# Reordering the first stage of a streaming trunk step: norm, conditioning and first projections

## What is computed

```python
mod = jax.nn.silu(c) @ w_ada + b_ada            # c: one row for the prompt, one for the sample
sh1, sc1, g1, sh2, sc2, g2 = jnp.split(mod, 6, axis=-1)
y = xf * lax.rsqrt(jnp.mean(xf * xf, axis=-1, keepdims=True) + EPS)   # rmsnorm, times gain
h = h * (1 + scale[:, None, :]) + shift[:, None, :]                   # modulate
rq, rk, rv, rg, aq, ak, av = split_in(h @ w_in)
```

## Time and profile before

| | us |
|---|---|
| time, median of 3 runs | 1336.36 |
| lowest and highest run | 1335.98 and 1337.28 |
| the profiled execution, its own time | 1338.92 |
| its span, from first to last instruction | 1337.1 |
| PE busy in the span | 1257.2 (94%) |
| DVE busy | 840.5 (63%) |
| ACT busy | 524.1 (39%) |
| POOL busy | 517.7 (39%) |

### The profile page before, as it was taken

How to read it: one execution, slowest core, us unless ns; L and a number is a source line. 1 busy time by engine, 2 the same in 40 slices (tenths; PEclk the granted TensorE clock), 3 DMA queues, 4 the chain that set the end, 5 groups by cost and what they waited for, 6 DMA issues and landing times.

```text
span 1337.1 us, 22495 instructions
## 1 busy us (share of the span) xinstructions
PE 1257.2 (94%) x8537; PEld 1181.3 (88%) x8537; DVE 840.5 (63%) x1519; ACT 524.1 (39%) x1063; POOL 517.7 (39%) x313
## 2 busy tenths in 40 slices
PE   5879999999999899779999999999999999999995
PEld 2548988988988899769999999999999999899995
DVE  5978558477396636996666666666666368682305
ACT  5644344345345523543343333334333322333432
POOL 0002032131042433444534535344352577665770
PEclk9999999999999899989999999999999999999998
DMA  9412223032222413203222232322222898685981
GB/s 366 168 53 80 72 73 125 24 120 78 92 90 89 151 36 115 99 32 116 102 109 98 99 114 90 122 98 99 106 91 85 310 365 302 217 325 200 321 274 45
DMA packets 74393, 185.56 MB, mean 139 GB/s; under 512 B 7424, under 2 KB 39744, under 8 KB 74048
## 3 DMA queue, kind: packets, MB, share of 16 engines
q1 hardware_dynamic: 72640, 183.63, 38.3%
q10 hardware_dynamic: 1664, 0.72, 0.2%
HBM read 150.14 MB, written 34.19 MB: 138 GB/s over the span
## 4 chain that ended last, share of the span: by engine, by line
PE 67%; DVE 12%; DMA 6%; POOL 5%; issue 5%; ACT 3%; SPq 2%; DVEq 0%; ACTq 0%; POOLq 0%
PE bank L2166 32%; PE bank L1893 13%; PE bank L2206 9%; PE bank L2142 5%; DMA w_raw<-in_w_units 4%; POOL w_extra L1295 2%; PE bank L2013 2%; DVE std L1530 1%; DVE ada_out L1332 1%; PE bank L1983 1%; POOL w_more L1295 1%; PE bank L1998 1%; POOL w_hl L1295 1%; POOL w_hl L1256 1%; DMA ada_d<-in_w_ada_t 1%
## 5 line engine op out<-in xcount | busy, mean ns | idle before, releaser
L1893 PE MATMUL bank<-act_hl,w_hl 128*128 128x362 f32 (+1 forms) x1368 | 256.5, 336 | 0.1
L1893 PEld LDWEIGHTS bank<-act_hl,w_hl 128*128 128x128 f32 x1368 | 223.3, 188 | 9.4 <-issue 7.1
L1183 POOL TENSOR_TENSOR w_hl<-w_raw,w_hl 128x1024 fp32r<-128x1024 f32 x21 | 50.2, 2392 | 345.1 <-ACT w_hl L727 345.1
L2206 PE MATMUL bank<-u_hl,w_more 128*128 128x362 f32 (+1 forms) x672 | 116.3, 332 | 4.4 <-POOL w_more L1295 4.1
L2166 PE MATMUL bank<-x_blocks_a,w_hl 128*128 128x272 f32 x864 | 114.0, 291 | 5.8 <-issue 5.8
L2206 PEld LDWEIGHTS bank<-u_hl,w_more 128*128 128x128 f32 x672 | 113.5, 191 | 5.1 <-POOL w_more L1295 4.5
L2166 PEld LDWEIGHTS bank<-x_blocks_a,w_hl 128*128 128x128 f32 x864 | 111.6, 191 | 6.1 <-issue 6.0
L2166 PE MATMUL bank<-x_blocks_b,w_hl 128*128 128x272 f32 x864 | 112.7, 288 | 1.4 <-ACT x_blocks_b L993 1.1
L2166 PE MATMUL bank<-x_blocks_a,w_ext 128*128 128x272 f32 x840 | 109.5, 289 | 4.3 <-DVE prod_sb L1635 2.4
L2166 PEld LDWEIGHTS bank<-x_blocks_b,w_hl 128*128 128x128 f32 x864 | 109.8, 188 | 2.3 <-DVE up_b L1640 1.3
L2166 PEld LDWEIGHTS bank<-x_blocks_a,w_ext 128*128 128x128 f32 x840 | 106.8, 189 | 5.0 <-issue 2.6
(11 more groups left out here) (229 smaller groups left out, 2290.2 us busy)
## 6 DMA issues: line engine op xcount, KB each, us to landing
w_raw<-in_w_units SPq DMA_DIRECT2D x139, 512.0 KB, 4.5
ada_w<-in_w_ada_t SPq DMA_DIRECT2D x36, 512.0 KB, 3.6
u_hl<-u_dram SPq DMA_DIRECT2D x44, 362.0 KB, 5.6
u_dram<-acc SPq DMA_DIRECT2D x22, 544.0 KB, 2.7
u_dram<-up_b SPq DMA_DIRECT2D x22, 544.0 KB, 2.7
ada_d<-in_w_ada_t SPq DMA_DIRECT2D x16, 512.0 KB, 5.8
u_hl<-u_dram SPq DMA_DIRECT2D x22, 364.0 KB, 7.7
xm<-in_x_t SPq DMA_DIRECT2D x2, 1448.0 KB, 13.8
```

Source lines behind the costliest of these rows:

```text
L1183: pool.tensor_tensor(w_hl[:, slot, 1], w_raw[:, slot], w_hl[:, slot, 0].bitcast(F32), ALU.subtract).then_inc(wl_ready, 1)
L1893: ins = pe.matmul(bank[c][:, 0:m], w_hl[:, slot, w, k, :], act_hl[:, x, k, a:a + m], start=(pas == 0 and i == 0), stop=(pas == 2 and i == ...
L2206: ins = pe.matmul(bank[o][:, 0:m], w_down(q)[:, w, o, :], u_hl[:, q % U_RING, x, 0:m], start=(f == pas == 0), stop=(f == FT - 1 and pas == 2))
```

## The change

`std_flat` now takes the roots without the two spare columns, so that all 1088 reciprocals lie side by side. A list X_STEPS takes the place of X_ORDER: rows 0 and 1 by chunks, rows 2 to 6 in one step over all tokens (instructions of 1024 and 64 columns), row 7 by chunks. ACT shifts in place only, and PE waits for that (`x_shifted`); the rounded high part becomes a separate copy of a whole row (`x_hi`), some steps later. On DVE the dots of tiles 4, 5, 6 and 7 move ahead, between and behind the three reciprocals. On PE row 7 is worked chunk by chunk as its chunks come, the ninth product waits for one result copied out instead of seven, and the nine transpositions go to three banks without a wait between them, after the eighth result is copied; DVE copies them in three instructions. ACT copies results in the order in which they are made.

```diff
--- before.py
+++ after.py
@@ -75,8 +75,9 @@
 W_RING = W_MORE + 3 + W_EXTRA
 ADA_LOADS = tuple(range(11))
 ADA_PLACE = {m: m % 11 for m in range(16)}
-X_ORDER = ([(0, 0), (1, 0), (0, 1), (1, 1), (2, 0), (2, 1), (0, 2), (1, 2), (2, 2)]
-           + [(k, c) for k in range(3, KT) for c in range(3)])
+X_STEPS = ([(k, lo, hi) for ks, c in (((0, 1), (0, 1)), ((0, 1), (2,))) for k in ks for lo, hi in
+            [(CHUNKS[i][0], sum(CHUNKS[i])) for i in c]] + [(k, 0, T) for k in range(2, KT - 1)]
+           + [(KT - 1, a, a + n) for a, n in CHUNKS])
 LATE = 4
 OUT_JOBS = ([(o, n) for o in range(1, 8) for n in (0, 1)] + [(o, n) for o in (4, 5, 3, 7) for n in (2, 3)]
@@ -228,6 +229,7 @@
+        X_LAST = [max(i for i, step in enumerate(X_STEPS) if step[0] == k) for k in range(KT)]
@@ -265,6 +267,7 @@
+        x_shifted = sem("x_shifted")
@@ -742,15 +745,19 @@
                 act.activation(std[:, c, 0:n], bank[at or SUM_BANK[c]][:, 0:n], ACT.Sqrt, bias=eps_sb[:, 0:1],
                                scale=1.0 / width).then_inc(std_ready, 1)
-            def shift_x(k, c):
-
-                act.wait_ge(x_scaled, X_ORDER.index((k, c)) + 1)
-                for in_place in (False, True):
-                    for o, tok, m, part in pieces(c):
-                        x = xm[:, k, tok:tok + m]
-                        ins = act.activation(x if in_place else act_hl[:, 0, k, tok:tok + m], x, ACT.Identity,
-                                             bias=mod[:, 2 * k + 1, part:part + 1])
-                ins.then_inc(hi_ready, 1)
+            def shift_x(i):
+
+                k, lo, hi = X_STEPS[i]
+                act.wait_ge(x_scaled, i + 1)
+                for o, tok, m, part in token_parts(lo, hi):
+                    x = xm[:, k, tok:tok + m]
+                    ins = act.activation(x, x, ACT.Identity, bias=mod[:, 2 * k + 1, part:part + 1])
+                ins.then_inc(x_shifted, 1)
+
+            def x_hi(k):
+
+                act.wait_ge(x_shifted, X_LAST[k] + 1)
+                act.activation(act_hl[:, 0, k, :], xm[:, k, :], ACT.Copy).then_inc(hi_ready, 1)
             act.sem_inc(state_stored, 32)
             act.sem_inc(wh_ready, 3)
@@ -768,7 +775,7 @@
             def x_root(c):
                 n = CHUNKS[c][1]
                 act.wait_ge(sum_ready, c + 1)
-                act.activation(std[:, c, 0:n], bank[X_SUM_BANK[c]][:, 0:n], ACT.Sqrt, bias=eps_sb[:, 0:1],
+                act.activation(std_flat[:, CHUNKS[c][0]:sum(CHUNKS[c])], bank[X_SUM_BANK[c]][:, 0:n], ACT.Sqrt, bias=eps_sb[:, 0:1],
                                scale=1.0 / D).then_inc(std_ready, 1)
             act.wait_ge(cond_loaded, 16)
@@ -780,8 +787,14 @@
             x_squares(2)
             x_root(2)
             act.wait_ge(sq_used, 3 * KT)
-            for k, c in X_ORDER:
-                shift_x(k, c)
+            for i in range(len(X_STEPS)):
+                shift_x(i)
+                if 6 <= i <= 10:
+                    x_hi(i - 6)
+                if i == 10:
+                    x_hi(5)
+                    x_hi(6)
+            x_hi(KT - 1)
             def evac(n_chunk, at, dst, func=ACT.Copy, scale=1.0):
@@ -790,20 +803,27 @@
                 act.activation(dst[:, a:a + n], bank[at][:, 0:n], func, scale=scale).then_inc(act_evac, 1)
             for c in range(3):
-                act.wait_ge(gemm_ready, c + 1)
-                for o, t, n, part in pieces(c):
-                    ins = act.activation(ak[:, t + P * part:t + P * part + n], bank[c][:, o:o + n], ACT.Copy)
-                ins.then_inc(act_evac, 1)
-            act.wait_ge(act_evac, 3)
+                for u in range(3):
+                    if u == c == 2:
+                        continue
+                    act.wait_ge(gemm_ready, 3 * c + u + 1)
+                    for o, t, n, part in pieces(c):
+                        if u == 0:
+                            ins = act.activation(ak[:, t + P * part:t + P * part + n], bank[c][:, o:o + n], ACT.Copy)
+                        elif part == 0:
+                            a, n = CHUNKS[c]
+                            ins = act.activation((rv, aq)[u - 1][:, a:a + n], bank[3 * u + c][:, 0:n], ACT.Copy,
+                                                 scale=(1.0, ATT_SCALE)[u - 1])
+                    ins.then_inc(act_evac, 1)
+            split_weights(3, [3])
+            act.wait_ge(act_evac, 7)
             act.dma_start(pk_t, ak[:, S_PROMPT - P:S_PROMPT]).then_inc(stored, 16)
             act.dma_start(sk_t, ak[:, T + P - S_SAMPLE:T + P]).then_inc(stored, 16)
-            for c in range(3):
-                evac(3 + c, 3 + c, rv)
-            split_weights(3, [3])
-            for c in range(3):
-                evac(6 + c, (6, 7, 0)[c], aq, scale=ATT_SCALE)
+            act.wait_ge(gemm_ready, 9)
+            a, n = CHUNKS[2]
+            act.activation(aq[:, a:a + n], bank[0][:, 0:n], ACT.Copy, scale=ATT_SCALE).then_inc(act_evac, 1)
             split_weights(4, [4])
-            act.wait_ge(av_tok_ready, NB)
+            act.wait_ge(av_tok_ready, 3)
             act.dma_start(pv, av_tok[:, 7, :]).then_inc(stored, 16)
             act.dma_start(sv, av_tok[0:S_SAMPLE, 9, :]).then_inc(stored, 16)
@@ -1365,12 +1385,19 @@
                                   ALU.add, ALU.mult).then_inc(vec_ready, 1)
                 dve.wait_ge(vec_ready, k + 1)
-            def scale_x(*parts):
-
-                for k, c in parts:
-                    for o, tok, m, part in pieces(c):
+            def first_invert(c):
+
+                at = std_flat[:, CHUNKS[c][0]:sum(CHUNKS[c])]
+                dve.wait_ge(std_ready, c + 1)
+                then_wait(dve.reciprocal(at, at))
+
+            def scale_x(*steps):
+
+                for i in steps:
+                    k, lo, hi = X_STEPS[i]
+                    for o, tok, m, part in token_parts(lo, hi):
                         x = xm[:, k, tok:tok + m]
-                        ins = dve.scalar_tensor_tensor(x, x, scale_n[:, 0, k, part:part + 1], std[:, c, o:o + m],
+                        ins = dve.scalar_tensor_tensor(x, x, scale_n[:, 0, k, part:part + 1], std_flat[:, tok:tok + m],
                                                        ALU.mult, ALU.mult)
                     ins.then_inc(x_scaled, 1)
@@ -1380,40 +1407,42 @@
                                   ALU.subtract).then_inc(lo_ready, 1)
             dve.wait_ge(silu_c_ready, 1)
-            for m in range(4):
+            for m in range(5):
                 first_ada_dots(m)
-            invert(0, 0)
+            first_invert(0)
+            for m in (5, 6):
+                first_ada_dots(m)
+            first_invert(1)
             first_vectors(0)
-            scale_x((0, 0))
+            scale_x(0, 1)
             first_vectors(1)
-            scale_x((1, 0))
-            first_ada_dots(4)
-            first_ada_dots(5)
-            invert(1, 1)
-            scale_x((0, 1), (1, 1))
+            scale_x(2, 3)
+            first_invert(2)
+            scale_x(4, 5)
             first_vectors(2)
-            scale_x((2, 0), (2, 1))
-            invert(2, 2)
-            scale_x((0, 2), (1, 2), (2, 2))
-            for k in range(3, KT):
+            scale_x(6)
+            first_ada_dots(7)
+            first_vectors(3)
+            scale_x(7)
+            for k in range(4, KT):
                 first_ada_dots(2 * k)
                 first_ada_dots(2 * k + 1)
                 first_vectors(k)
-                scale_x(*[(k, c) for c in range(3)])
-
-            dve.wait_ge(x_scaled, 3 * KT)
+                scale_x(*[i for i, step in enumerate(X_STEPS) if step[0] == k])
+
+            dve.wait_ge(x_scaled, len(X_STEPS))
             dve.sem_inc(norm_applied, 3)
-            dve.wait_ge(hi_ready, 3 * (KT - 1))
-            for k in range(KT - 1):
+            for k in range(KT):
+                dve.wait_ge(hi_ready, k + 1)
                 x_lo(k)
-            dve.wait_ge(hi_ready, 3 * KT)
-            x_lo(KT - 1)
-
-            for b in range(NB):
-                t, n = BLOCKS[b]
-                dve.wait_ge(av_t_ready, b + 1)
-                dve.tensor_copy(av_tok[0:n, b + (b == NB - 1), :], bank[(3, 6)[b % 2]][0:n, 0:P]).then_inc(av_tok_ready, 1)
+
+            for i, (b0, b1) in enumerate(((0, 4), (4, 8))):
+                dve.wait_ge(av_t_ready, i + 1)
+                dve.tensor_copy(av_tok[:, b0:b1, :], bank[(3, 6)[i]][:, :].rearrange("p (b d) -> p b d", b=4)).then_inc(
+                    av_tok_ready, 1)
+            dve.wait_ge(av_t_ready, 3)
+            dve.tensor_copy(av_tok[0:S_SAMPLE, NB, :], bank[4][0:S_SAMPLE, 0:P]).then_inc(av_tok_ready, 1)
             def mask_and_max(j, b):
@@ -1924,14 +1953,6 @@
             def nothing(s):
                 pass
-            def values_by_token(s):
-
-                t, n = BLOCKS[s]
-                if s >= 2:
-                    pe.wait_ge(av_tok_ready, s - 1)
```

(31 more changed lines are left out.)

## The result

The changed kernel takes 1324.51 us (median of 4 runs, 1324.09 to 1325.66), against 1336.49 us for the kernel before on the same chips. The ratio is 0.9911, with a 95% interval from 0.9899 to 0.9922: 12.0 us faster, where 11.6 were forecast. Two later measurements, each beside the kernel before, gave 11.1 and 10.5 us. Its profiled execution took 1324.34 us, with a span of 1322.5.

A forecast was written before the change was run, and what follows sets the result against it. DVE's chain bounds the first stage, though PE leads overall. Unit 3 starts 11.6 us earlier (5.4 from DVE's chain, the rest PE's last row, clock, ninth product and transpositions, less POOL's hold): 1336.36 to 1324.8 us, range 1321.5 to 1329.0.

The forecast's parts named there:

- DVE up to the last row: DVE's chain before unit 3: idle pieces go and whole rows cost 1.40 us, so row 7 starts 5.4 us earlier.
- PE and the last row: PE before unit 3: the 4.46 us wait goes, row 7 takes 5.15 us from 73.3, transpositions end at 84.9.
- the reason given for it: PE's row 7: charged 5.15 us because the lower clock followed an idle PE that would no longer be idle.
- What is late next: Low parts on DVE before unit 3: held by POOL's subtraction, they end at 86.1, after the transpositions; unit 3 starts then.
- one hold by POOL: DVE's low parts: POOL's subtraction for unit 3's weights takes a turn among them, moving their end 2.4 us from 83.7.
- rival 1: Before unit 3: no hold between POOL and the low parts, unit 3 at 84.9, 1323.6 us; chance 0.20.
- Behind unit 3: From unit 3's start to the end: the change costs nothing, and weight loads move with the rest.
- rival 2: DVE's whole rows: they bring nothing because columns cost all, 1.3 us lost, 1326.1 us; chance 0.10.
- Rival 3: The heads: a load or table of the first head becomes late, time stays at about 1336 us; chance 0.04.
- Rival 4: DVE's dots before roots: tile 5 or 6 landing late delays the chain, slower if tile 6 lands after 39.0; chance 0.02.

The follow-up runs named there:

- dots_behind: Changed kernel, but DVE's dots of tiles 4 to 6 go back behind the roots; 1330.97 us.
- rows_by_chunks: Changed kernel, but rows 2 to 6 are scaled and shifted chunk by chunk instead of whole; 1328.44 us.
- by_turns: Changed kernel, but the nine transpositions take turns in two banks again, each waiting for the copy before the last; 1330.47 us.
- subtraction_later: Changed kernel, but POOL's first subtraction also waits for six low parts, so it comes up during the seventh; 1325.53 us.
- late_wait_for_low: Changed kernel, but PE waits for low parts only behind unit 3's first eight products and first scores; DVE copies values before its last low part; 1324.04 us.
- no_subtraction: Changed kernel, but POOL leaves out its first subtraction, so the low part of unit 3's weights is zero; 1323.12 us.
- tile_6_late: Changed kernel, but SP issues the loads of conditioning tiles 6 and 7 behind the three weight units; 1329.75 us.
- last_row_whole: Changed kernel, but row 7 is scaled, shifted and waited for as a whole, like rows 2 to 6; 1327.33 us.
- early_and_late: Kernel of late_wait_for_low, but ACT loads its table early by a one-column Silu and SP issues conditioning tile 4 before x chunk 1; 1324.02 us.

## Why the prediction was right

**DVE up to the last row.** Right step by step: reciprocal 0 at 22.52 (22.4 forecast), vectors 0 at 32.5 (32.4), rows 3, 4 and 7 scaled at 44.01, 51.03 and 72.13 (44.0, 51.0, 72.1). A whole row costs 1.39 (1.40). The run dots_behind shows that the order of the dots is worth some 5 us at unit 3 (of the 5.7 to 6.1 us, 0.9 are a root that came later), and rows_by_chunks that whole rows are worth 1.3.

**PE and the last row.** Row 7 was forecast to start at 73.3 and started at 73.42; the ninth product at 78.86 (78.5), the end of the transpositions at 84.96 (84.9), nine of them in 1.15 us (1.3). One thing came otherwise: row 5, from 61.02 us, took 6.84 us, so the stretch at the lower clock was still there, after an idle PE of 1.89 us. It was hidden, since row 6 was not ready before 68.06. In the third run of the changed kernel it came in row 6 (the granted clock is 0.53 of full speed from 69 to 71 us, 0.62 from 71 to 73 and 1.00 after), which pushed row 7 back by 1.2 us; rows 6 and 7 took 11.72 us together, the transpositions ended at 85.80, and unit 3 started there, no later than in the others. So row 7 itself was spared in all three profiles, but the reason given for it was only half right. PE's waits of 1.9 us did not go; they moved to rows 5 and 6, and in by_turns, subtraction_later and late_wait_for_low two of them were followed by rows of 5.15 us. Which row is slowed differs between profiles of one kernel, and that it was none that mattered is partly luck.

**What is late next.** The low parts with one hold by POOL were forecast to end at 86.1; DVE's next instruction starts at 85.80 and PE at 86.22. Two small errors cancel in it: the hold was charged 2.4 us and cost 2.15, and PE started 0.34 us after the last low part ended (74.02 + 11.86 = 85.88), where the sum had nothing. That the hold is POOL's is shown by no_subtraction (84.80, the forecast of rival 1 being 84.9). The Trainium skill, "SBUF — State Buffer", section "SBUF: two separate sides", has the two blocking each other for whole instructions, and a low part of 3.44 instead of 1.28 us, 2.16 more, with a subtraction of 2.4 in between, agrees. DVE's copies of values, forecast at most 0.2 us late, ended at 87.27, before the first scores began at 87.74.

**Behind unit 3.** "Nothing" was right within what the profiles can tell: the rest of the span is 1236.3 to 1239.8 us for the changed kernel and 1239.45 for the one before. A change of 1 us there could not be seen. That the first median hit the forecast to 0.3 us is therefore luck in part: the second and third are 1.2 and 2.0 us above 1324.8. What carries the prediction is the start of unit 3, 11.4 to 11.9 us earlier where 11.6 was forecast.

**The rivals.** Rival 1 (no hold) and rival 2 (columns cost all) fall by the profile and by a run each. Rival 3 (the heads give it back) falls by the time. Rival 4, dots in front of roots made late by a load, did not happen, but tile_6_late shows its mechanism: 3.6 us of load are 3.6 us at unit 3.

**The reserve.** Why does PE's part of the change look small when it is undone? Because two paths end almost together. The last row by chunks and the separate rounding move PE's path, and each can be undone alone for 0 to 0.5 us. The transpositions without waits are another matter: undone, they cost 2.5 us, since the copies that they wait for stand behind the low parts. The ninth product's wait was not undone alone. Before the change that path ended at 97.65, with the low parts finished at 89.09: PE's edits brought it down to the low parts, and the last microsecond of them is now slack. How much each of them took off on the way is not shown, since no run undoes two together.

## What to carry to other kernels

Instructions that wait for nothing belong in front of those that wait for another engine; count then when their own data land, since a queue that works in order passes on each microsecond of a late load (3.6 here). When several edits shorten one path until it meets another, undoing one of them tells little: read where both paths end. And measure from an event behind the first loads, not from the start of the span: here that took the spread of the changed kernel from 0.42 us to 0.04. Before a POOL instruction is moved into a run of DVE instructions with two inputs in SBUF, add their durations up, as one after the other.

## What was not expected of the hardware

Who waits for whom, POOL or DVE, followed a pattern that I can't explain. In eight profiles POOL's subtraction came up during the sixth of the eight low parts (as at 80.09 above), and the seventh was held. In four (tile_6_late, last_row_whole, subtraction_later and the third run of the changed kernel) it came up during the seventh, and the eighth ran at once, so that POOL's instruction lasted 3.9 to 4.6 us. It is not simply that the last instruction of a run goes first, or that copies stand behind it: in late_wait_for_low and early_and_late, two of the eight, only seven low parts stood in front of the copies, and the seventh and last was held all the same (3.44 us from 81.01 in the former). What decides it stays open. Its cost is the same either way, as unit 3 waits for both.
